# Two parts of an operand in one matmul of 512 columns, and their halves summed by VectorE

## What is computed

```python
def swiglu(h, w_gate, w_up, w_down):
    return (jax.nn.silu(h @ w_gate) * (h @ w_up)) @ w_down

x = x + swiglu(rms_norm_2(x, norm_ffn[i]), ffn_w_gate[i], ffn_w_up[i], ffn_w_down[i])
```

## Time and profile before

| | us |
|---|---|
| median of 3 runs (1170.75 to 1172.44) | 1171.16 |
| the profiled execution | 1171.18 |
| its span, first to last instruction | 1169.9 |
| TensorE busy | 1121.0 (96%) |
| VectorE busy | 733.6 (63%) |
| ScalarE busy | 579.7 (50%) |

### The profile page before, as it was taken

The page is one execution under the profiler, slowest core; times in us unless marked ns, Lnnn a source line. Parts: engine busy times, 40 slices in busy tenths (PEclk is TensorE's granted clock), DMA queues, the critical chain, the costliest instruction groups (busy, mean ns, idle before and its releaser), DMA issues.

```text
span 1169.9 us, 16512 instructions
## 1 busy us (share of the span) xinstructions
PE 1121.0 (96%) x6899; PEld 1004.0 (86%) x6899; DVE 733.6 (63%) x965; ACT 579.7 (50%) x822; POOL 49.2 (4%) x82
## 2 busy tenths in 40 slices
PE   2699999999999998999999999999999999999997
PEld 2688988788889986898999998788888989999986
DVE  5766665575777997655566554455886546555643
ACT  2447754344564652654535444445764545444441
POOL 3021000000000000000100000000011000000000
PEclk9899999899999999999999999999999999999999
DMA  9796434455546403543554554655345435546450
GB/s 345 259 294 186 150 132 133 154 195 168 198 161 199 144 1 108 180 138 115 152 178 171 191 194 164 216 170 175 124 144 175 149 108 194 180 150 215 140 184 37
DMA packets 105884, 195.17 MB, mean 167 GB/s; under 512 B 6106, under 2 KB 22642, under 8 KB 105809
## 3 DMA queue, kind: packets, MB, share of 16 engines
q1 hardware_dynamic: 103248, 187.51, 47.7%
q0 software_dynamic: 2560, 6.60, 2.0%
HBM read 193.04 MB, written 1.05 MB: 166 GB/s over the span
## 4 chain that ended last, share of the span: by engine, by line
PE 82%; DVE 10%; ACT 4%; DMA 1%; issue 1%; POOL 0%; SPq 0%; DVEq 0%; ACTq 0%; POOLq 0%
PE product L577 73%; DVE conv_out L2399 4%; ACT w_high L506 2%; DVE w_low L516 1%; DMA w_raw<-in_w_ada 1%; DVE gain L532 1%; PE small L695 1%; PE small L1873 1%; PE small L1245 1%; PE small L1256 1%; PE small L610 1%; PE small L1894 1%; PE small L2642 1%; PE small L2658 0%; PE small L1266 0%
## 5 line engine op out<-in xcount | busy, mean ns | idle before, releaser
L516 DVE TENSOR_TENSOR w_low<-w_raw,w_high 128x2048 fp32r<-128x2048 f32 (+3 forms) x172 | 377.5, 2198 | 232.6 <-ACT w_high L506 230.8
L506 ACT ACTIVATE w_high<-w_raw 128x2048 fp32r<-128x2048 f32 (+3 forms) x172 | 315.0, 1836 | 177.7 <-PE product L577 159.4
L577 PE MATMUL product<-H_low,w_high 128*128 128x256 f32 x1080 | 309.5, 287 | 10.2 <-DVE w_low L516 9.2
L577 PE MATMUL product<-H_high,w_low 128*128 128x256 f32 x1080 | 307.5, 285 | 0.0
L577 PE MATMUL product<-H_high,w_high 128*128 128x256 f32 x1080 | 307.0, 284 | 0.0
L577 PEld LDWEIGHTS product<-H_low,w_high 128*128 128x128 f32 x1080 | 208.8, 193 | 12.0 <-DVE w_low L516 9.7
L577 PEld LDWEIGHTS product<-H_high,w_low 128*128 128x128 f32 x1080 | 209.0, 193 | 0.3
L577 PEld LDWEIGHTS product<-H_high,w_high 128*128 128x128 f32 x1080 | 208.8, 193 | 0.0
L577 PE MATMUL product<-w_high,H_low 128*128 128x512 f32 (+2 forms) x384 | 152.0, 396 | 0.0
L577 PE MATMUL product<-w_low,H_high 128*128 128x512 f32 (+2 forms) x384 | 149.5, 389 | 0.0
L577 PE MATMUL product<-w_high,H_high 128*128 128x512 f32 (+2 forms) x384 | 149.1, 388 | 0.0
(11 more groups left out here) (376 smaller groups left out, 1475.0 us busy)
## 6 DMA issues: line engine op xcount, KB each, us to landing
w_raw<-in_ffn_w_gate SPq DMA_DIRECT2D x20, 1024.0 KB, 5.1
w_raw<-in_ffn_w_up SPq DMA_DIRECT2D x20, 1024.0 KB, 5.2
w_raw<-in_ffn_w_down SPq DMA_DIRECT2D x20, 1024.0 KB, 5.0
w_raw<-in_w_merge SPq DMA_DIRECT2D x16, 1024.0 KB, 5.1
w_raw<-in_w_ada SPq DMA_DIRECT2D x12, 1024.0 KB, 8.6
w_raw<-in_w_in SPq DMA_DIRECT2D x8, 1024.0 KB, 6.6
w_raw<-in_mem_w_k SPq DMA_DIRECT2D x8, 1024.0 KB, 5.1
w_raw<-in_conv_w_pw SPq DMA_DIRECT2D x16, 512.0 KB, 4.7
```

The source lines that it names most:

```text
L506: k.act.eng.activation(chunk_view(k, k.w_high[j], i), chunk_view(k, k.w_raw[i % k.N_RAW], i), ACT.Copy).then_inc(*k.act.tells("weights_hig ...
L516: k.vec.eng.tensor_tensor(low, raw, high.bitcast(F32), ALU.subtract).then_inc(*k.vec.tells("weights_low", ("weights low", i)))
L577: mm = pe.eng.matmul(bank[:, off:off + wide], a, r, start=b not in started, stop=True, skip_group_check=True)
```

## The change

`H` becomes one buffer with the high parts of all tiles, then the low parts, so that a view `parts[:, :, tile, :]` has 2 x 256 columns, 8 KB apart. A new `pe_apart` replaces `pe_block` for gate and up products 1 to 4 of both layers. Each of the four groups of 128 features gets a bank of its own. For each tile of depth one matmul with the high weights takes both parts of H, 512 columns, high in the bank's first half and low in its second; a second one, of 256 columns, adds low weights x high H to the first half. The gate product uses the four `product` banks, the up product the four `small` banks. VectorE sums the halves of a bank by a TENSOR_REDUCE over a view with the halves innermost (`add_parts`): in `gates_apart` into `mid`, which is then multiplied by the roots; in `ups_apart` all four into new buffers `up_sums`, which `mid` is then multiplied by. The first product (`both`), the last narrow one and the down product stay as they were.

```diff
--- before.py
+++ after.py
@@ -249,7 +249,8 @@
 
 
     def __init__(self, name, parts, before=None):
-        self.name, (self.high, self.low), self.before = name, parts, before
+        self.name, (self.high, self.low, *parts), self.before = name, parts, before
+        self.parts = parts[0] if parts else None
 
     def ready(self, chunk):
         return ("ready", self.name, chunk)
@@ -345,7 +346,8 @@
         self.gains_at = self.at
         self.gains = [self.sb(f"gain{i}", [P, D]) for i in range(2)]
         self.stats, self.stat_at, self.st = self.sb("stats", [P, 728]), 0, {}
-        h = self.pair("H", KT)
+        parts = self.sb("H", [P, 2, KT, S], F32R)
+        h = parts[:, 0, :, :], parts[:, 1, :, :], parts[:, :, :, :]
         names = ["first", "merged", "conv", "ln", "mem0", "ffn0", "kv", "q", "att", "mem1", "ffn1"]
         ops = {name: Operand(name, h, before) for before, name in zip([None, *names], names)}
         self.H_first, self.H_merged, self.H_conv, self.H_ln, self.H_kv, self.H_q, self.H_att = (
@@ -439,6 +441,7 @@
         hidden = self.pair("hidden", FT)
         self.hidden = [Operand(f"hidden{layer}", hidden) for layer in range(2)]
         self.mids = self.ring("mid", 2, [P, CK, S])
+        self.up_sums = [self.sb(f"up_sums{b}", [P, 2, S]) for b in range(2)]
         self.ffn_diagonal, self.ffn_roots = self.sb("ffn_diagonal", [P, NT, P]), self.sb("ffn_roots", [P, S])
         self.positions, self.lambda_rows = self.sb("positions", [P, NT], I32), self.sb("lambda_rows", [P, 4, HD])
 
@@ -590,6 +593,29 @@
 
 
 FEATURES = [(i // 2, S * (i % 2), None, P * i, P) for i in range(CK)]
+
+
+def pe_apart(k, key, ring, x):
+
+
+    pe = k.pe
+    for b in range(CK):
+        ring.take((key, b))
+    for step, first in enumerate(range(0, KT, CK)):
+        i = pe.chunk
+        pe.chunk += 1
+        high, low = (chunk_view(k, t[i % k.N_SPLIT], k.split[i]) for t in (k.w_high, k.w_low))
+        pe.wait_ge(("weights low", k.split[i]), x.ready(step))
+        for b in range(CK):
+            bank, column = ring.of((key, b)), slice(b * P, (b + 1) * P)
+            if step == 0:
+                pe.wait_ge(ring.before((key, b)))
+            for j in range(CK):
+                pe.eng.matmul(bank[:, :].rearrange("p (i n) -> p i n", n=S), high[:, j, column], x.parts[:, :, first + j, :], start=first + j == 0,
+                              stop=True, skip_group_check=True)
+                mm = pe.eng.matmul(bank[:, 0:S], low[:, j, column], x.high[:, first + j, :], start=False, stop=True, skip_group_check=True)
+        mm.then_inc(*pe.tells("products", ("products", key), ("multiplied", i), x.taken(step)))
+        yield step
 
 
 def pe_columns(k, key, x, tiles, inside={}, early={}):
@@ -2044,8 +2070,8 @@
             pe.eng.matmul(bank[:, 0:S], k.ones, k.ffn_diagonal[:, :, :].rearrange("p t n -> p (t n)"), start=True, stop=True).then_inc(
                 *pe.tells("spread", key))
     for n in range(1, FULL):
-        drain(pe_block(k, ("ffn gate", layer, n), H, KT, FEATURES))
-        drain(pe_block(k, ("ffn up", layer, n), H, KT, FEATURES))
+        drain(pe_apart(k, ("ffn gate", layer, n), k.product, H))
+        drain(pe_apart(k, ("ffn up", layer, n), k.small, H))
     drain(pe_block(k, ("ffn last", layer), H, KT, FEATURES))
     after = k.norms["after", layer]
     for n in range(D // CN):
@@ -2139,6 +2165,34 @@
             V.eng.tensor_tensor(at, at, ps, ALU.mult).then_inc(*V.tells("hidden", ("hidden", layer, f), k.product.free(bank)))
             V.wait_ge(("hidden", layer, f), ("hidden high", layer, f))
             V.eng.tensor_tensor(lo, at, hi.bitcast(F32), ALU.subtract).then_inc(*V.tells("operand_low", hidden.ready(f // CK), k.mids.free((layer, n))))
+
+    def add_parts(ring, key, f, dst, *ready):
+
+        bank = ring.of((key, f))
+        V.wait_ge(("products", key), *ready)
+        V.eng.tensor_reduce(dst, bank[:, :].rearrange("p (i n) -> p n i", n=S), AX.X, ALU.add).then_inc(*V.tells("parts_added", ring.free((key, f))))
+
+    def gates_apart(n, key):
+        slot = k.mids.take((layer, n))
+        for b in range(2):
+            at = mid_view(slot, b)
+            for i in range(2):
+                add_parts(k.product, key, 2 * b + i, at[:, i, :], k.mids.before((layer, n)))
+            V.wait_ge(V.last)
+            V.eng.tensor_tensor(at, at, two_roots, ALU.mult).then_inc(*V.tells("scaled", ("scaled", layer, n, b)))
+
+    def ups_apart(n, key):
+        slot = k.mids.of((layer, n))
+        for b in range(2):
+            for i in range(2):
+                add_parts(k.small, key, 2 * b + i, k.up_sums[b][:, i, :])
+        for b in range(2):
+            f, hidden, at = CK * n + 2 * b, k.hidden[layer], mid_view(slot, b)
+            hi, lo = hidden.high[:, f:f + 2, :], hidden.low[:, f:f + 2, :]
+            V.wait_ge(V.last, ("gated", layer, n, b))
+            V.eng.tensor_tensor(at, at, k.up_sums[b][:, :, :], ALU.mult).then_inc(*V.tells("hidden", ("hidden", layer, f)))
+            V.wait_ge(("hidden", layer, f), ("hidden high", layer, f))
+            V.eng.tensor_tensor(lo, at, hi.bitcast(F32), ALU.subtract).then_inc(*V.tells("operand_low", hidden.ready(f // CK), k.mids.free((layer, n))))
     for step in range(4):
         vec_chunk(k)
         key = ("both", layer)
@@ -2157,11 +2211,10 @@
             ups(0, ("products", key, 3), [(key, 2), (key, 3)])
     next(beside, None)
     for n in range(1, FULL):
-        for part, name in ((gates, "ffn gate"), (ups, "ffn up")):
+        for part, name in ((gates_apart, "ffn gate"), (ups_apart, "ffn up")):
             vec_chunk(k)
             vec_chunk(k)
-            key = (name, layer, n)
-            part(n, ("products", key), [(key, 0), (key, 1)])
+            part(n, (name, layer, n))
         next(beside, None)
     vec_chunk(k)
     vec_chunk(k)
```

## The result

The changed kernel takes 1174.3 us (median of 20 runs, 1171.5 to 1175.8) against 1169.5 us of the kernel before in the same sets (20 runs, 1167.2 to 1172.4): ratio 1.0037, 95% interval 1.0030 to 1.0043. It is slower by 0.37%, some 4.4 us. Forecast were +3.8 us, a ratio of 1.0033, and 1175.0 us on a base of 1171.16 us.

A forecast was written before the change was run, and what follows sets the result against it. TensorE, busy 96% of the span, bounds the kernel, but the change makes VectorE's ring the longer one. Layer 0 +4.68, layer 1 -1.15 and clock +0.3 give +3.8 us, 1175.0 us; range 1170.5 to 1182.

The forecast's parts named there:

- VectorE's ring: VectorE reads banks, ScalarE works, both split the next weights: a round of 23.25 us per n, against TensorE's 22.24.
- TensorE's saving: Gate and up products 1 to 4: 32 chunks at 5.56 us instead of 5.76, at most 6.4 us saved.
- Rival (d): 512-column matmuls save nothing, 5.76 us a chunk: +5.5 to +6 us, 1177 us; chance 0.66 together with the forecast.
- A reduction: Each of 64 added VectorE TENSOR_REDUCE takes 0.69 us, the next starting 0.61 us later if nothing holds it.
- rival (c): The 256 outputs or the stride make a VectorE reduction cost 0.96 us: +20 us, 1191 us; chance 0.08.
- rival (a): VectorE's round fits into TensorE's, with a reduction at 0.424 us: -3.6 us, 1167.6 us; chance 0.08.
- Rival (b): VectorE's round a little shorter, by a reduction at 0.66 us or overlap: +1.5 to +2 us, 1173 us; chance 0.18.
- Layer 1: Its feed-forward stage: 3.20 us saved on TensorE, 2.05 lost in stalls of 0.43, 1.01 and 0.61, so -1.15 us.
- Layer 0: Its feed-forward stage, with angles and an exponential in the round: stalls of 4.6, 3.0, 1.1 and 0.6, so +4.68 us.
- The stop behind the exponential: In layer 0, TensorE waits for weights delayed by the exponential after the second up product: a stall of 3.0 us.
- The clock: After the 4.6 us stall in layer 0 the granted clock may drop to 1.2 GHz: 0 to +0.6 us, +0.3 taken.
- Costed at nothing: Weight loads and the four banks never stall TensorE; VectorE's backlog of 5 us is worked off in the down products.

The follow-up runs named there:

- the kernel with 8 spare products: Changed kernel with 8 unneeded float32 matmuls issued on TensorE ahead of its 4.12 us wait before ups 2 of layer 0: 1174.0 us, 1.0035.
- matmuls alone: Kernel with the changed matmuls but without the sums, VectorE multiplying only the first half of each bank: 1166.3 us, 0.9970 of the kernel before.
- ScalarE earlier: Changed kernel with only ScalarE splitting weights one chunk earlier, VectorE's and TensorE's programs untouched: 1168.5 us, 0.9986 of the kernel before.
- both engines earlier: Changed kernel with ScalarE and VectorE both splitting weights one chunk earlier: 1173.0 us, 1.0024 of the kernel before.
- sums alone: Kernel before, its matmuls kept, plus eight reductions for each n on VectorE into buffers nobody reads: 1176.1 us, 1.0052.

## Why the prediction was right

It said slower by 3.8 us through VectorE's ring, and the measured 4.4 come that way: VectorE's round is longer than TensorE's, TensorE stops behind `w_low` in layer 0, layer 1 gains a little. The sum was nearer than its terms, since some errors cancel. That it came within 0.6 us of the measured difference is in part luck.

- **TensorE's saving** was put at 0.20 us a chunk from the denser of two rows. Layer 1 without any wait is 101.97 us; two narrow chunks of 5.76 less, that is 5.65 for each of 16, a saving of 0.11. The forecast kept 5.64 as its upper case, from 232.6 ns a matmul, and that row was the right one. Rival (d), no saving, is ruled out by the same figures, though its time would have been near. The most that the change can give is 3.4 us and not 6.4. This was the largest error of a term, and it hardly moved the sum, because the late splits set when the stretch ends, and a TensorE that is slower only waits less for them: three stops in layer 0 where four were forecast, and one at the end of layer 1 instead of three.
- **A reduction** was put at 0.69 and 0.61 from start to start. It takes 0.68 and 0.60. The stride and the 256 outputs cost nothing that the rows show, which was rival (c), and the reads, not the writes, set the time, against rival (a). From the first up operation to the end of the next split it is 10.19 us (forecast 10.22), from the first gate operation 8.73 (8.77).
- **The ring** is 23.15 (23.25) against 4 x 5.65 = 22.60 (22.24) of TensorE. The loss per n is 0.55, not 1.01. Rival (b), a ring a little shorter, came true in this figure, but not in the time.
- **Layer 1**: -1.15 forecast, -1.17 measured. Saved 1.71 (forecast 3.20), lost 0.54 (2.05). The two errors of 1.5 us are one and the same: the stretch ends when VectorE's last split is ready, and what TensorE saves less it waits less. That this end was met to 0.02 us (102.53 forecast, 102.51 measured) is luck: VectorE starts ups 1 at 22.81 us, 0.30 later than forecast, and its three rounds are 0.10 shorter each.
- **Layer 0**: +4.68 and 0.3 for the clock were forecast, +5.56 measured. The stretch without waits would be 101.97, so 8.80 are lost: 5.5 in the three stops, the rest by the 0.27 us of run-out that each of them has ahead of it and, most of it, by the slow clock after the first. The later stages follow the forecast's times with a shift of about 1 us: ups 3 and 4 start at 77.38 and 100.5 us, forecast 76.28 and 99.53. The stop behind the exponential was forecast at 3.0 us and took 1.07, since TensorE came to it late, most of all by the slow clock. The forecast put the kernel before at 105.12 us; its trace has 105.21.
- **The clock** was the term sized too low: 0 to 0.6 us, 0.3 taken. VectorE starts ups 2 at 52.34 us, where the kernel in which the clock stayed up has 51.15: 1.2 us. The forecast had 51.7 as its upper end, by TensorE restarting at 37.96, two chunks of 5.56 and a loss of 2.3. Measured are a restart at 38.22, chunks of 5.65, and 14.12 us from the restart to VectorE's start, of which 2.5 are left for the clock when two chunks and 0.27 are taken off. Each of these is a little above its forecast, and together they are the 0.64 between 51.7 and 52.34. At the end of the stretch the clock costs some 1.0 us, the estimate from the kernel with 8 spare products, whose ups 3 and 4 start at 76.41 and 99.57 us, nearly as forecast without the clock. So the terms of layer 0 without the clock were right within 0.1 us, and the 0.58 us by which layer 0 missed are the 0.7 by which the clock was sized too low, less that 0.1. The forecast also saw no second dip: keeping the first one away gained only 0.4 us, since TensorE then stopped longer at the next split.
- **Costed at nothing**: loads and banks. No wait of TensorE for either shows in the two stages; all its waits there name `w_low`. The down product works off the backlog as assumed: from its first matmul on the kernel takes 310.27 us to layer 1's stretch and 68.55 to the end, before 310.15 and 68.47.

The Trainium skill, page "VectorE: DVE Perf Modes", section "The perf-mode tier table", lists only the 1× mode for `tensor_reduce`, whatever the memory. The trace agrees: its 512 inputs from PSUM take 0.68 us, within 0.01 of the 512 of a multiplication (0.69), for a strided view and with 256 outputs too. By the table in its section on the TRN2 errata this operation would take, as an estimate, 658 ns; it took 681, and the measurement decides.

What stays open: whether the sums could be left to an instruction that doesn't stand in VectorE's ring at all. ScalarE has time (49% busy), but its splits stand in the same ring, and this wasn't tried.

## What to carry to other kernels

When each engine works a hand-written order, cost an edit by the round of the ring it is put into, not by busy shares: VectorE at 63% of the span before the change looked like ample room, and yet 5.2 us of new VectorE time per n (2.52 behind the gates, 2.65 behind the ups) made VectorE's round the longer one by 0.55 us. Look next for the other work that lived on that ring's slack, since it pays first: here the same angles and exponential cost 1.5 us before and 8.2 after. And before taking an edit of this kind back, look at who waits for whom in the order: against the changed kernel, shifting ScalarE against VectorE gave 6 us, shifting both alike between 1 and 2.

## What the runs showed of the hardware

- Granted clock after a stop of TensorE in layer 0, read from windows of 2 us in seven of these kernels: 1.00 after stops of 1.3 us (before), 1.64 (matmuls alone) and 1.96 (ScalarE earlier); it falls behind stops of 2.16 (8 spare products, two windows at 0.57 and 0.58), 2.70 (both engines earlier, three at 0.50), 3.91 (sums alone, 0.62 and 0.52) and 4.12 (changed, three at 0.50). Such a stop cost twice, as idleness and as slow work behind it. Whether the length of the stop alone decides, these runs don't show. The forecast had looked only at the 5.57 us of the earlier trace rows.
- 512 moving columns of H and 256 more take 0.353 us from start to start, with the two halves 8 KB apart; the two together are 320 ns of columns at 2.4 GHz, so some 16 ns a matmul are left, where one of 256 alone had 13. Sixteen matmuls fewer in a chunk should save 0.21 us by the 13 ns, and saved 0.11.
- Costs of parts in a ring don't add. By the stretches the sums alone are +5.08 us and the matmuls alone -3.05, which would be +2.0; together they are +4.4. What the matmuls save, TensorE spends waiting for the same splits.
